# Turning six activation operands with VectorE blocks and SBUF moves instead of TensorE transposes

## The reference

```python
h = rms_norm(x, g0);  parts = split(h @ w_in)          # four mixers: GLA, FNet, Hyena, short conv
x = x + concat(mixers(parts)) @ w_out                  # "x2" in the kernel
q = rms_norm(x, g1) @ w_xq;  k, v = split(rms_norm(mem, gm) @ w_xkv)
x = x + softmax(q k^T / sqrt(512)) v @ w_xo            # "x3"
gate, up = split(rms_norm(x, g2) @ w_gate_up)          # 2048 -> 2 x 5632
x = x + (silu(gate) * up) @ w_down                     # product "ff", result "x4"
x = rms_norm(x, g_final)
u = rms_norm(x, ga) @ a_w_in;  a, b, z = split(u)      # conformer layer
y = silu(layer_norm(causal_conv31(a * sigmoid(b)))) * silu(z)
x = x + y @ a_w_out                                    # "x5"
k, v = split(rms_norm(x, gkv) @ w_kv)                  # last layer: differential attention
q, z = split(rms_norm(x, gb) @ b_w_in)
x = x + (rms_norm(diff_attention(q, k, v)) * silu(z)) @ b_w_out
```

## Time and profile before

| | before |
|---|---|
| median of 3 runs | 2383.76 us (2382.84 to 2384.13) |
| profiled execution | 2382.62 us |
| its span, first to last instruction | 2380.8 us |
| TensorE matmuls busy | 2366.8 us, 99%, 10794 matmuls |
| VectorE busy | 1379.4 us, 58% |
| ScalarE busy | 1112.9 us, 47% |
| GpSimd busy | 320.8 us, 13% |
| moved by DMA | 440.65 MB, mean 185 GB/s |

### The profile page before, as it was taken

How to read it: one execution, slowest core, us unless ns; L and a number is a source line. 1 busy time by engine, 2 the same in 40 slices (tenths; PEclk the granted TensorE clock), 3 DMA queues, 4 the chain that set the end, 5 groups by cost and what they waited for, 6 DMA issues and landing times.

```text
span 2380.8 us, 26679 instructions
## 1 busy us (share of the span) xinstructions
PE 2366.8 (99%) x10794; PEld 1935.1 (81%) x10794; DVE 1379.4 (58%) x1835; ACT 1112.9 (47%) x1426; POOL 320.8 (13%) x256
## 2 busy tenths in 40 slices
PE   9999999999999999999999999999999999999999
PEld 6777778888888888888888888888888888877887
DVE  5676756544445554454454555669984565456554
ACT  6433646444334444443344444544556544444653
POOL 1111010000000000000000000049987000011100
PEclk9999999999999999999999999999999999999999
DMA  9575446565435655555555555555655555654454
GB/s 336 190 234 156 157 158 229 178 193 194 154 129 177 212 184 187 194 190 192 192 187 193 195 183 188 188 184 177 195 178 182 188 177 182 193 173 141 152 169 140
DMA packets 218188, 440.65 MB, mean 185 GB/s; under 512 B 9711, under 2 KB 9898, under 8 KB 217361
## 3 DMA queue, kind: packets, MB, share of 16 engines
q1 hardware_dynamic: 213328, 421.88, 53.7%
q0 software_dynamic: 4736, 17.06, 2.2%
HBM read 432.64 MB, written 2.10 MB: 183 GB/s over the span
## 4 chain that ended last, share of the span: by engine, by line
PE 95%; DVE 2%; ACT 1%; DMA 1%; issue 0%; SPq 0%; POOL 0%; DVEq 0%; ACTq 0%; POOLq 0%
PE ps L96 93%; PE ps L99 3%; DMA RAW<-in_w_in 1%; DVE WLO L108 1%; ACT WHI L102 1%; SPq L134 0%; DVE ST L119 0%; DVE Alo L116 0%; POOL ST L108 0%; DVE ED L108 0%; DVE ND L116 0%; ACT WIN L102 0%; ACT BB L102 0%; ACT Ahi L102 0%; ACT L102 0%
## 5 line engine op out<-in xcount | busy, mean ns | idle before, releaser
L108 DVE TENSOR_TENSOR WLO<-RAW,WHI 128x1024 fp32r<-128x1024 f32 x701 | 854.8, 1223 | 757.5 <-ACT WHI L102 753.1
L102 ACT ACTIVATE WHI<-RAW 128x1024 fp32r<-128x1024 f32 x793 | 837.8, 1059 | 898.8 <-PE ps L96 892.5
L96 PE MATMUL ps<-WHI,Ahi 128*128 128x512 f32 x1904 | 754.1, 396 | 2.4 <-DVE Alo L116 2.0
L96 PE MATMUL ps<-WHI,Alo 128*128 128x512 f32 x1904 | 741.3, 390 | 0.0
L96 PE MATMUL ps<-WLO,Ahi 128*128 128x512 f32 x1904 | 740.8, 389 | 0.0
L96 PEld LDWEIGHTS ps<-WHI,Ahi 128*128 128x128 f32 x1904 | 357.6, 188 | 83.2 <-issue 6.3
L96 PEld LDWEIGHTS ps<-WHI,Alo 128*128 128x128 f32 x1904 | 357.4, 188 | 75.2
L96 PEld LDWEIGHTS ps<-WLO,Ahi 128*128 128x128 f32 x1904 | 357.7, 188 | 74.7 <-issue 2.9
L113 POOL TENSOR_SCALAR ST<-ST 128x1 f32<-128x1 f32 (+3 forms) x53 | 21.3, 401 | 1710.9 <-DVE ST L119 1441.1
L108 POOL TENSOR_TENSOR WLO<-RAW,WHI 128x1024 fp32r<-128x1024 f32 x92 | 218.9, 2405 | 54.6 <-ACT WHI L102 54.2
L116 DVE SCALAR_TENSOR_TENSOR ps<-YT,GC,ps 128x256 f32<-128x256 f32 x480 | 188.8, 485 | 8.0 <-ACT ps L102 8.0
(11 more groups left out here) (307 smaller groups left out, 2058.9 us busy)
## 6 DMA issues: line engine op xcount, KB each, us to landing
RAW<-in_w_gate_up SPq DMA_DIRECT2D x88, 1024.0 KB, 5.0
RAW<-in_a_w_in SPq DMA_DIRECT2D x48, 1024.0 KB, 5.1
RAW<-in_w_down SPq DMA_DIRECT2D x44, 1024.0 KB, 5.0
RAW<-in_w_in SPq DMA_DIRECT2D x39, 1024.0 KB, 6.4
RAW<-in_w_xkv SPq DMA_DIRECT2D x32, 1024.0 KB, 5.4
RAW<-in_w_kv SPq DMA_DIRECT2D x32, 1024.0 KB, 5.4
RAW<-in_b_w_in SPq DMA_DIRECT2D x32, 1024.0 KB, 5.3
RAW<-in_w_out SPq DMA_DIRECT2D x16, 1024.0 KB, 5.0
```

The lines of the kernel that those rows point to most:

```text
L96: return self.e.matmul(o, l, r, start=start, stop=stop, skip_group_check=True)
L102: return self.e.activation(o, i, func, scale=scale, **kw)
L108: return self.e.tensor_tensor(o, a, b, op)
```

## The change

For x2, x3, x4, x5 and ff the TensorE transposes go. In their place:

- `swap` on VectorE turns a quarter of X (128 x 512, for both position tiles), or AC, in 32x32 blocks with its own block transpose, into a staging tile T (4 KB per partition): two instructions for each of 27 swaps.
- `move` on SyncE carries the blocks to the partitions where they belong, from T to a home tile B (for ff the home is AC itself): 16 DMAs for each swap, each 32 partitions x 2 x 512 bytes (32 KB). It waits for the swap, and (not for ff) until the quarter before has been split.
- `moved_hi` and `moved_lo` read the home tile in SBUF instead of PSUM, in runs of 32 elements, one instruction for each k, where for ff one instruction did two.
- x5 is turned once; x5b takes its high and low part from the same home tile in the same step. For that the places of Dhi, Dlo, DKT and Ohi in SBUF are exchanged.
- The steps sit later: the split of a quarter behind halves 4 and 5 of its chunk instead of 0 and 1 (ff: half 5), and the swap ahead of its half 0. For x5: swaps at ("co", 1) 6, ("co", 2) 4, ("co", 3) 2 and ("dk", 0) -1, splits from ("co", 2) 2, ("co", 3) 0, ("co", 3) 6, ("dk", 0) 4.
- SyncE's program now walks `line` too, since the moves have their places in it; pieces are loaded on the same events as before.
- The scaling of X for the last norm of the first block (`x4scale`) also waits for the last swap of x4.

```diff
+    SWAP = {"x2": (at("T2", AR + 64, [1024]), at("B2", AR + 68, [1024])),
...
+             "x5": (at("T5", AR + 80, [1024]), at("B5", AR + 54, [1024])),
+             "ff": (at("TF", AR + 80, [1024]), flat(AC))}
+    def turned_blocks(stage, t):
+        return SWAP[stage][0][:, :].rearrange("p (q t k c) -> p q t k c", q=4, t=2, k=4)[:, :, t]
+    def moved(stage, k):
+        return SWAP[stage][1][:, :].rearrange("p (b k c) -> p k b c", b=8, k=4)[:, k % 4]
...
-        put_each(n, 0, [("x3T", 4 * i), ("x3T", 4 * i + 2)])
+        put(n, -1, ("swap", "x3", i))
+        put_each(n, 4, [("x3T", 4 * i), ("x3T", 4 * i + 2)])
     for i in range(11):
-        put(("down", 0, 0) if i == 5 else ("down", 6, 0) if i == 10 else ("gate", i + 1), 0, ("ffT", i))
+        n = ("down", 0, 0) if i == 5 else ("down", 6, 0) if i == 10 else ("gate", i + 1)
+        put(n, -1, ("swap", "ff", i))
+        put(n, 5, ("ffT", i))
...
+    for i, n, j, m, k in ((0, ("co", 1), 6, ("co", 2), 2), (1, ("co", 2), 4, ("co", 3), 0),
+                          (2, ("co", 3), 2, ("co", 3), 6), (3, ("dk", 0), -1, ("dk", 0), 4)):
+        put(n, j, ("swap", "x5", i))
+        put_each(m, k, [("x5T", 4 * i), ("x5T", 4 * i + 2)])
...
+        def moved_hi(stage, k):
+            home = "x5" if stage == "x5b" else stage
+            hi, n = SPLIT[stage][0], split_slot(stage, k)
+            for b in range(4):
+                e.wait_ge(*of(f"d_move{b}", home, k // 4, 3))
+            for j in range(2):
+                i = e.activation(by_block(hi[:, n + j, :]), moved(home, k + j), scale=GAIN[stage](k + j) if stage in GAIN else 1.0)
+            i.then_inc(*done("T_hi", stage, k))
...
+        def swap(stage, i):
+            n = SWAPS.index((stage, i))
+            if n:
+                for b in range(4):
+                    e.wait_ge(*of(f"d_move{b}", *SWAPS[n - 1], 3))
...
+            e.wait_ge(*(evicted(("up", i)) if stage == "ff" else of("x_add", stage, i, 1)))
+            for t in range(2):
+                a = AC[:, t, :] if stage == "ff" else X[:, t, i * 512:(i + 1) * 512]
+                m = e.turn_blocks(turned_blocks(stage, t), a.rearrange("p (k q c) -> p q k c", k=4, q=4))
+            m.then_inc(*done("swapped", stage, i))
...
+        def move(stage, i):
+            turned, home = SWAP[stage]
+            e.wait_ge(*of("swapped", stage, i))
+            if i and stage != "ff":
+                e.wait_ge(*of("T_lo", "x5b" if stage == "x5" else stage, 4 * i - 2))
+            for b in range(4):
+                for q in range(4):
+                    to = home[32 * q:32 * q + 32, :].rearrange("p (t b n) -> p b t n", t=2, b=4)[:, b]
+                    e.dma_start(to, turned[32 * b:32 * b + 32, q * T:(q + 1) * T].rearrange("p (t n) -> p t n", t=2)) \
+                        .then_inc(*landed(f"d_move{b}", stage, i, q))
```

More of the change, by code:

```diff
@@ L493, in build_program @@
     put(("mo", 3), 6, ("spread",))
-    put_each(("xkv", 0), 0, [("x2T", k) for k in range(0, 16, 2)])
+    for i in range(4):
+        put(("xkv", i), -1, ("swap", "x2", i))
+        put_each(("xkv", i), 4, [("x2T", 4 * i), ("x2T", 4 * i + 2)])
     for i in range(4):
@@ L1342, in step @@
                 e.wait_ge(*full(("cz", 3)))
[L1343 to L1346, removed]
+                moved_hi("x5", k)
+                moved_hi("x5b", k)
             elif what == "mask":
@@ L1407, in t_lo, with moved_lo @@
             i.then_inc(*done("T_lo", stage, k))
+        def moved_lo(stage, k):
+            home = "x5" if stage == "x5b" else stage
+            (hi, lo), n = SPLIT[stage], split_slot(stage, k)
+            e.wait_ge(*of("T_hi", stage, k))
+            for j in range(2):
+                o, m, h = by_block(lo[:, n + j, :]), moved(home, k + j), by_block(f(hi[:, n + j, :]))
+                if stage in GAIN:
+                    i = e.stt(o, m, GAIN[stage](k + j), h, AL.mult, AL.subtract)
+                else:
+                    i = e.tensor_tensor(o, m, h, AL.subtract)
+            i.then_inc(*done("T_lo", stage, k))
+        def swap(stage, i):
[3 more added lines that the diff above has]
+                    e.wait_ge(*of(f"d_move{b}", *SWAPS[n - 1], 3))
+            home_free = {("x2", 0): of("mem_sq", 1), ("x3", 0): of("pa", ("att", 3)), ("x5", 0): of("pa", ("zT", 14)), ("ff", 0): of("pa", ("qxT", 14))}
+            if i == 0 and (stage, i) in home_free:
+                e.wait_ge(*home_free[stage, i])
+            e.wait_ge(*(evicted(("up", i)) if stage == "ff" else of("x_add", stage, i, 1)))
[3 more added lines that the diff above has]
+            m.then_inc(*done("swapped", stage, i))
         def add_x(name, stage, i):
@@ L1744, in step @@
                 t_lo("x1", k, pa, ("x1", k))
+            elif what == "swap":
+                swap(*a)
             elif what == "sarg":
@@ L2096, in sp_program @@
             load_piece(q)
[L2097 to L2105, removed]
+        begun = 0
+        for h, (name, part, _) in enumerate(line):
+            if part == 0:
+                for what, *a in behind.get((name, -1), ()):
+                    if what == "swap":
+                        move(*a)
+            while begun <= ahead(h):
+                n = halves[begun][0] + 4
+                if piece_end(n - 4) == begun and n < len(pieces):
+                    e.wait_ge(*of(*lo_event(begun)))
+                    if n in (8, 9):
+                        t = n - 8
+                        e.dma_start(X[:, t, :], I["x"][0, t * P:(t + 1) * P, :]).then_inc(*landed(f"d_x{t}", 0))
+                    load_piece(n)
+                begun += 1
+            for what, *a in behind.get((name, part), ()):
+                if what == "swap":
+                    move(*a)
         for i in range(4):
```

57 lines of the change are left out of this document (23 added, 34 removed).

## The result

The changed kernel takes 2372.16 us (median of 4 runs, 2370.68 to 2374.83) against 2383.59 before (4 runs, 2382.84 to 2384.13): 0.9952 of the time, 95% interval 0.9936 to 0.9968. That is faster, as the forecast had it, but by 11.4 us where 27.4 were forecast, and 2 us above the range. All 29.4 us of turns went. In the profiled execution, which is the slowest of the four and whose span is 7.8 us shorter than before, this came in their place: about 14 us of new waits of TensorE and about 6 us of a lower granted clock behind them, most of both in the loop of the last layer, and 1.7 us of a lower clock ahead of anything the change touches. Two steps of the prediction failed. The issue of a move was mis-sized: it is 0.64 us from start to start, not 0.42. And with that size three swaps of the last layer, whose room the prediction hadn't worked out, don't fit.

The account below looks back on a forecast made before the run. TensorE, busy 2366.8 of 2380.8 us, was taken as the bound. Removed turns 29.4 less stalls of 0, 0.5 (x4) and 1.5 (x5) gave a gain of 27.4, so 2356.4 us; range 2352.5 to 2370.

Parts of the forecast that it names:

- 248 turns gone: TensorE's queue: removing 160 turns of X and 88 of AC saves 29.4 us, with one VectorE wait.
- Landing 1.9: Moves from T to B: each was taken to land in 2 us, with 1.8 and 8.5 kept as bounds.
- x2 and ff free: x2, wanted 8 chunks later, and ff, wanted only from half 8 or 10, were to cost 0.
- a late quarter in x3, x4 and x5: Last quarter, wanted in halves 6 and 7: x3 room 1.8, cost 0; x4 cost 0.5; x5 cost 1.5 us.
- D: TensorE's turns are filler hiding another limit, so removing them gives nothing: 2383.8 us; chance 0.04.
- E: The moves don't overlap: 16 take 29 us at each of 27 swaps, over 300 us slower; chance 0.01.
- The prediction's own sign of being wrong: Forecast wrong if TensorE's idle time grows by more than 10 us or the matmuls' pitch is not 0.227.
- I take 0.42, the settled issue and its gap: SyncE's queue: each move costs 0.42 us to issue, so 16 take 6.7 us per swap.
- The bounds of 0.37 and 0.97: Range kept for one move's issue on SyncE, in us; the upper is the longest issue and a gap.
- x5 is dearer: Last layer: x5b is cast in the same steps, k = 14 comes about 1 late; cost put at 1.5 us.
- Rival B: Moves land after 8.5 us, stalls 19 instead of 2: 2373.4 us; sign: ScalarE waits 5 us or more; chance 0.14.
- C's limit of 0.70: SyncE's queue: above 0.70 us per issue, each swap delays the next weight piece; at 0.97, 2471 us; chance 0.08.

Follow-up runs that it names:

- the kernel with both repairs: The changed kernel with half of the moves issued by GpSimd, plus two home tiles and six or five halves from swap to split for x5: 2353.05 us.
- the spaced swaps: The changed kernel, all moves still on SyncE, with two home tiles for x5, earlier swaps and later splits: 2360.43 us.

## Why the prediction was wrong, and where it was right

*Right, step by step.* 248 turns gone, at 0.49 per four and 0.87 per eight: the kernel with both repairs has the whole of it back. Matmul pitch 0.2268. Block turn 0.69, forecast 0.69. Landing 1.9, forecast 2. x2 and ff free; the convolution unchanged (194.94 of 217 us of VectorE, as in the earlier trace rows). That the danger was a late quarter in x3, x4 and x5, in front of Alo of k = 12 or 14: so it came in x3 and x4. Rivals D and E are out: no turn was filler, and the moves overlap, one starting every 0.64 us and landing in 1.9. (The 2.0 us that E adds up from the Trainium skill, "DMA: Bandwidth & Descriptors", Anatomy of one DMA, are given there for DMAs issued by GpSimd, and these came from SyncE.) The prediction's own sign of being wrong did show: TensorE's idle time grew by 13.9 us, more than 10.

*Wrong 1, the size: "I take 0.42, the settled issue and its gap".* It is 0.597 + 0.04 = 0.64 us. The 0.42 is one issue behind one other; from 2.6 to 5.5 us in the same start-up of the kernel before stand issues of 0.45 to 0.64, which the prediction left out. The 0.368 of weights was no guide for two reasons. It is of issues that each stand alone: here a weight issue right behind a move takes up to 587 ns. And a move is dearer even alone: the first of a swap takes 0.59. The bounds of 0.37 and 0.97 held the price, and the 0.55 on GpSimd lay near it; I took a value from the low end. By the prediction's own formulas, with 3.5 us more to issue: x3 late by 3.5 - 1.8 = 1.7 (measured 1.19), x4 by 0.5 + 3.5 = 4.0 (2.18).

*Wrong 2, what was left out: three of the four swaps of the last layer.* "x5 is dearer" was worked out for the last swap alone: 1.5, and with the 3.5 it is 5.0. The first three have four halves of room, 10.9 us (of these the prediction has only the third, as casts that "begin when the moves land" and hold up the last add by 2 us). At 0.42 the chain is 1.3 + 6.7 + 2 = 10.0 and fits by 0.9; at 0.64 it is 1.3 + 10.3 + 1.9 = 13.5 and misses by 2.6, three times: 7.8. So the wrong size crossed an edge that the prediction hadn't looked at. With both mended the sum is 29.4 - 1.7 - 4.0 - 12.8 = 10.9, and 2383.8 - 10.9 = 2372.9, which is the measured 2372.16 to 0.7 us. That closeness is in part luck, for the parts fit less well: the waits of the last layer are 10.5 and not 12.8, the first of the three late quarters costs TensorE nothing, those of x4 are 2.2 and not 4.0, and the clock's 5.7 are not in it.

*Wrong 3, the clock.* I charged a wait at its length. In the last layer 10.5 us of waits came with 5.7 more beside a lower granted clock; behind the waits of x3 and x4, of 1.0 to 1.2 us each, it stayed at 1.00.

*The rivals.* Rival B gives 2373.4, near the measured time, but not by its mechanism: ScalarE does wait up to 7 us for B, its sign, but the moves land in 1.9, not 8.5. What arrives late is the last of them, because it was issued late. C's limit of 0.70 was not reached; the new waits for late weight pieces are ScalarE's 7.2 us for w_gate_up and 5.0 for w_down, none of which reaches TensorE (there is no gap in the 702.04 us), and the doubling of the moves showed that another wait decides before it.

## What to carry to other kernels

Price a burst of DMAs by issues of the same form that stand behind each other in the same queue, not by the median issue of a stream of other DMAs that has gaps; then add swap, burst and landing in a row and hold them against the room of every use, each turn of a loop apart and not the last alone. Where a burst is on the path, splitting it over two queues helps if the second engine has nothing due, and a queue shared with the bulk loads also keeps these off the DMA engines while the burst lands.

## What was not expected of the hardware

- A move's issue on SyncE took 0.59 us, the first of a swap as well as those behind it, plus 0.04 between them. Behind another it was 0.59 whether it moved 32 or 16 KB in 512-byte rows or 32 KB in 1 KB rows; first of its swap it was 0.51 for the latter two. A weight piece's issue took 0.368 alone and 0.587 right behind a move. On ScalarE a move's issue took 0.622, beside SyncE's own, and on GpSimd 0.533 to 0.536.
- 32 KB from SBUF to SBUF landed in 1.8 to 1.9 us with the DMA engines at a share of 0.2 to 0.3, and in 4.4 (median of 432) from GpSimd with weights running beside; where 1 MB loads ran beside both queues, SyncE's took 5.1 and GpSimd's 5.0.
- At TensorE's waits of 3.63, 3.15 and 2.53 us in the last layer the granted clock fell to the lower level (1.2 GHz) for 3.4 us each time, 1.5 to 1.7 us lost; at the wait of 1.18 between them and at those of 1.01 to 1.19 in x3 and x4 it stayed at 1.00. A single wait of 2.58 us, with the spaced swaps, cost the same 1.7.
